# Forming the low parts of four weight units of each mixer on GpSimd in place of VectorE, in a two-layer hybrid backbone on one Trainium2 core

## The reference

```
p_ctx = h_ctx @ w_in
p_lat = h_lat @ w_in
...
z_c, xs_c, b_c, c_c, dtr_c = ssm_inputs(p_ctx[..., o2:], conv_w, conv_b)
...
out_lat = jnp.concatenate([oa_l, ob_l, oc_l], axis=-1)
...
xl = xl + ml[5] * (mix_l @ w_out[l])
```

## Time and profile before

| | |
|---|---|
| median of 3 runs | 1856.92 us (1856.59 to 1858.24) |
| the profiled execution's own time | 1856.45 us |
| its span, first to last instruction | 1854.7 us |
| busy: PE, PEld, DVE, ACT, POOL | 1802.6 (97%), 1490.1 (80%), 1426.0 (77%), 750.3 (40%), 59.8 us (3%) |
| mean granted TensorE clock | 0.976 |
| PE's waits for the mixer's low parts (L961) | 9.1 us, in 3 waits, the longest 4.4 us |

### The profile page before, as it was taken

The page is one execution under the profiler, slowest core; times in us unless marked ns, Lnnn a source line. Parts: engine busy times, 40 slices in busy tenths (PEclk is TensorE's granted clock), DMA queues, the critical chain, the costliest instruction groups (busy, mean ns, idle before and its releaser), DMA issues.

```text
span 1854.7 us, 26139 instructions
## 1 busy us (share of the span) xinstructions
PE 1802.6 (97%) x9314; PEld 1490.1 (80%) x9314; DVE 1426.0 (77%) x2351; ACT 750.3 (40%) x1146; POOL 59.8 (3%) x104
## 2 busy tenths in 40 slices
PE   8999999999999899999999999999999998899999
PEld 5788888886776577888888888888888687599999
DVE  6899977889786767777878678777786988757665
ACT  4322222247745657222222362222224765754342
POOL 1000000000000000000000010000000000000000
PEclk8999999999998899999999999999999999979999
DMA  8445544413312023444443233444440323025542
GB/s 356 178 178 205 196 165 158 176 72 124 126 46 91 1 91 137 152 165 158 153 178 144 91 137 142 178 155 158 158 157 26 137 75 148 13 114 185 193 172 107
DMA packets 37587, 259.50 MB, mean 140 GB/s; under 512 B 4369, under 2 KB 5841, under 8 KB 7441
## 3 DMA queue, kind: packets, MB, share of 16 engines
q1 hardware_dynamic: 26066, 182.32, 26.9%
q0 software_dynamic: 11456, 76.32, 11.2%
HBM read 252.60 MB, written 5.24 MB: 139 GB/s over the span
## 4 chain that ended last, share of the span: by engine, by line
PE 87%; ACT 5%; DVE 5%; issue 2%; DMA 1%; POOL 0%; DVEq 0%; ACTq 0%; SPq 0%; POOLq 0%
PE ps L1559 25%; PE ps L1560 25%; PE ps L1561 25%; PE ps L1663 2%; PE ps L1871 1%; ACT w_hi L566 1%; PE ps L1599 1%; ACT n_t L617 1%; PE ps L1595 1%; DVE cv L1276 1%; DMA scale_w<-scale_in 1%; PE ps L1932 1%; PE ps L1836 1%; DVE w_lo L961 1%; PE ps L1685 1%
## 5 line engine op out<-in xcount | busy, mean ns | idle before, releaser
L1559 PE MATMUL ps<-h_hi,w_hi 128*128 128x512 f32 (+2 forms) x1792 | 661.9, 369 | 14.7 <-DVE w_lo L961 9.1
L1560 PE MATMUL ps<-h_lo,w_hi 128*128 128x512 f32 (+2 forms) x1792 | 654.4, 365 | 0.0
L1561 PE MATMUL ps<-h_hi,w_lo 128*128 128x512 f32 (+2 forms) x1792 | 653.7, 365 | 0.0
L1559 PEld LDWEIGHTS ps<-h_hi,w_hi 128*128 128x128 f32 (+1 forms) x1792 | 341.0, 190 | 76.7 <-issue 11.0
L1560 PEld LDWEIGHTS ps<-h_lo,w_hi 128*128 128x128 f32 (+1 forms) x1792 | 341.1, 190 | 54.9 <-issue 1.4
L1561 PEld LDWEIGHTS ps<-h_hi,w_lo 128*128 128x128 f32 (+1 forms) x1792 | 340.9, 190 | 55.1
L956 DVE TENSOR_TENSOR w_lo<-raw,w_hi 128x2048 fp32r<-128x2048 f32 x132 | 302.0, 2288 | 83.1 <-ACT w_hi L566 83.0
L1084 DVE SCALAR_TENSOR_TENSOR x_res<-ps,abg,x_res 128x256 f32<-128x256 f32 x584 | 248.6, 478 | 140.9 <-PE ps L1561 139.4
L566 ACT ACTIVATE w_hi<-raw 128x2048 fp32r<-128x2048 f32 x129 | 246.6, 1911 | 258.7 <-PE ps L1561 256.7
L979 DVE CUSTOM_DVE_ANT_0 mod_prod<-mod_raw,cb 128x1024 f32<-128x1024 f32 x256 | 301.5, 1220 | 0.2 <-DVE mod_t L983 0.2
L1559 PE MATMUL ps<-a_hi,w_hi 128*128 128x512 f32 (+1 forms) x640 | 233.2, 364 | 5.6 <-DVE x_res L1084 5.6
(11 more groups left out here) (238 smaller groups left out, 1698.2 us busy)
## 6 DMA issues: line engine op xcount, KB each, us to landing
raw<-ffn_in SPq DMA_DIRECT2D x132, 1024.0 KB, 4.8
mod_raw<-mod_in POOLq DMA_DIRECT2D x68, 1024.0 KB, 5.0
raw<-proj_in SPq DMA_DIRECT2D x20, 1024.0 KB, 4.8
raw<-out_w_in SPq DMA_DIRECT2D x8, 1024.0 KB, 4.9
x_spill<-x_res SPq DMA_DIRECT2D x2, 2048.0 KB, 8.0
x_res<-x_spill SPq DMA_DIRECT2D x2, 2048.0 KB, 8.3
scale_w<-scale_in POOLq DMA_DIRECT2D x4, 512.0 KB, 12.8
x_res<-x_in SPq DMA_DIRECT2D x2, 1024.0 KB, 11.6
```

The source lines that it names most:

```text
L1559: pe.matmul(dst, w_hi[:, slot, wsl], hi, start=first, stop=False)
L1560: pe.matmul(dst, w_hi[:, slot, wsl], lo, start=False, stop=False)
L1561: return pe.matmul(dst, w_lo[:, slot, wsl], hi, start=False, stop=last)
```

## The change

The low parts of units 3, 4, 5 and 6 of both mixers are taken out of VectorE's stream and put into GpSimd's, in `mixer_rows`: two ahead of the DMA of the decay totals and two behind it. Each waits for the unit's high part and for the low part before it. VectorE's low part of unit 7 waits for `lo_ready` to count unit 6.

```diff
+POOL_LOWS = (3, 4, 5, 6)
...
+            def low_parts(layer, units):
+                for m in units:
+                    pool.wait_ge(hi_ready, mix_base(layer) + m + 1)
+                    pool.wait_ge(lo_ready, mix_base(layer) + m)
+                    pool.tensor_tensor(w_lo[:, m % 3, :], raw[:, m % 2, :], w_hi[:, m % 3, :], ALU.subtract).then_inc(lo_ready, 1)
+
             def mixer_rows(layer):
...
                 if layer == 0:
                     pool.memset(st[:, 2:4, :], 0.0).then_inc(st_zero, 1)
+                low_parts(layer, POOL_LOWS[0:2])
                 pool.wait_ge(row_act, ROW_ACTS * (layer + 1))
                 pool.dma_start(tot_dram[layer], lam[0:16, 72:76]).then_inc(tot_out, 16)
+                low_parts(layer, POOL_LOWS[2:4])
                 pool.wait_ge(cv_ready, 6 * (layer + 1))
...
             def split_mix(layer, m):
+                if m in POOL_LOWS:
+                    return
                 n = P if m == DT_UNIT else UNIT
                 dve.wait_ge(hi_ready, mix_base(layer) + m + 1)
+                if m - 1 in POOL_LOWS:
+                    dve.wait_ge(lo_ready, mix_base(layer) + m)
                 tt(w_lo[:, m % 3, 0:n], raw[:, m % 2, 0:n], w_hi[:, m % 3, 0:n], ALU.subtract).then_inc(lo_ready, 1)
```

## The result

The changed kernel takes **1877.95 us** (median of 4 runs, 1877.16 to 1879.30) beside 1856.76 us for the kernel before on the same chip (4 runs, 1855.86 to 1858.24). The ratio is **1.0106, 95% interval 1.0092 to 1.0120**: slower by 21.2 us where 13.4 were forecast. The span of the profiled execution is 1876.2 us against 1854.7, the mean granted clock 0.973 against 0.976; PE is still busy for 96% of the span.

A forecast was written before the change was run, and what follows sets the result against it. PE, busy for 97% of the span, was taken to bound the kernel, so only its idle time counts. 3.6 + 6.8 + 3.0 = +13.4 us on the median gives 1870.3 us, range 1858 to 1880 us.

The forecast's parts named there:

- The lock: Mixer heads: a VectorE instruction with two SBUF inputs waits out any GpSimd instruction reading SBUF, and the reverse.
- Rival 1: Mixer heads: no lock for this instruction, VectorE gains 2.29 us per low part; about 1852.8 us, faster; chance 10%.
- Rival 2: Mixer heads: GpSimd needs under some 2.5 us per low part; 0 to +3 us, about 1858 us; chance 12%.
- Rival 3: Mixer heads: a waiting GpSimd gets the lock only when VectorE runs idle; some +29 us, 1886 us; chance 8%.
- The price of one low part: Mixer heads: one low part on GpSimd takes 3.8 us, two passes over the tile, between 1.89 and 5.7 us.
- term 1: First mixer's head: PE starts tile 7 at 466.7 against 463.04, waiting for an evacuation and a low part; +3.6 us.
- term 2: Second mixer's head: PE starts tile 8 at 1493.4 against 1486.64, behind a late evacuation; +6.8 us.
- term 3: Second mixer's head: PE's added waits bring one more stretch of 6.2 us at half clock; +3.0 us, between 0 and 3.
- What costs nothing: First mixer: unit 6's low part has 5.1 us of slack and GpSimd's DMAs queue some 6 us later, without loss.
- The rest of what costs nothing: First mixer: `etb` is read over 20 us behind its issue, the library load hides in GpSimd's idle time; no loss.

The follow-up runs named there:

- e3: Kernel before, all low parts on VectorE, plus a useless GpSimd subtraction behind the fourth, fifth and sixth high parts of each mixer; 1879.64 us, ratio 1.0116.
- e4: Kernel before, all low parts on VectorE, plus three useless GpSimd memsets behind the same three high parts of each mixer; 1859.42 us, ratio 1.0013.
- e7: Kernel before, all low parts on VectorE, plus two useless one-input GpSimd copies behind the same three high parts of each mixer; 1873.53 us, ratio 1.0082.
- e1: The change with unit 6's low part back on VectorE, only units 3, 4 and 5 on GpSimd; 1871.61 us, ratio 1.0072 to the kernel before.
- e2: Kernel before with only unit 6's low part of each mixer moved to GpSimd; 1864.88 us, ratio 1.0035.
- e9: Kernel before with the convolution's middle tap formed on ScalarE for four of six channel tiles, nothing on GpSimd; 1863.30 us, ratio 1.0019.
- e5: Kernel before with only unit 6's low part on GpSimd and all six row transfers behind VectorE's eighth low part; 1875.80 us, ratio 1.0094.
- e6: The change with each GpSimd low part split into four subtractions of 512 columns; 1872.67 us, ratio 1.0074 to the kernel before.
- e8: Kernel before with only unit 6's low part on GpSimd, two `etb` transfers ahead of it, four wide ones behind VectorE's eighth; 1866.81 us, ratio 1.0055.

## Why the prediction was right in sign and short in size

- **The lock** was right. The steps of VectorE with two SBUF tiles as inputs that run beside a GpSimd row last about as long as that row, in both mixers, and e3, e4 and e7 show that reading SBUF on GpSimd does it, not lateness, not GpSimd's being busy. Its condition was too narrow: TENSOR_SCALAR steps, which read one SBUF tile, are held as well (L1337, 4.76 us for 0.48, is the first step that the change stops, where the prediction had put the scan). Rivals 1, 2 and 3 did not come: no step with two SBUF tiles as inputs kept its length (L1298 at 495.75, which has one of its two tiles in PSUM, did, inside GpSimd's row from 492.16 to 496.78), GpSimd took 4.6 us and not under 2.5, and it started 0.08 us behind its high part (445.58 behind 443.60 + 1.90 on ScalarE).
- **The price of one low part** was mis-sized: 4.6 us, where I took 3.8 between bounds of 1.9 and 5.7. The Trainium skill's page GPSIMD Engine Reference, in Performance versus the Vector engine, gives 4.5 us; the trace agrees with it (4.51 to 4.71) and not with my two passes.
- **First mixer, term 1**: tile 7 starts at 468.92, which is 467.75 less the 1.17 us by which that execution was late from its start, against 463.04: +4.7 for +3.6. **Second mixer, term 2**: when the second mixer begins, the changed kernel is 11.30 us late (GpSimd's memset of `rows`, 1467.37 for 1456.07), so tile 8's 1505.81 is 1494.51 against 1486.64: +7.9 for +6.8. The price explains more than what was missing: between the prediction's own points for 3.8 and 5.7 us, a price of 4.6 would give +5.2 and +9.0. Tile 7 of the second mixer was foretold for 1486.1 and is at 1486.80.
- **The clock, term 3**: what the second head lost behind tile 8's start is 10.28 - 7.9 = 2.4 us in the change, 9.30 - 7.9 = 1.4 in e1 (whose tile 8 starts at 1499.66, and which comes to the second mixer 5.17 us late), for +3.0. The granted clock agrees: 6.2 us at 0.56 cost 6.2 x 0.44 = 2.7 us in the change, and at e1's 0.73 they cost 1.7.
- The errors of the three terms cancel: e1, which has all that they speak of, is at +13.4 in its heads and in its median. There tile 7 is 4.7 us late, 0.6 of it is made up before the first `z`, tile 8 is 7.9 late and 1.4 are lost behind it, for 3.6, 6.8 and 3.0. That the sum is met to a tenth of a microsecond is luck. It is luck in part, too, that the change's 1877.95 us lies in the range of 1858 to 1880: the upper end stands for a price of 5.7 us, and what brings the time near it is a cost that the prediction put at nothing.
- **What costs nothing** is the step that failed. The low part of unit 6 lies 5.1 us ahead of its use, that was so, and PE never waits for it. But its end also frees `raw`, and I did not follow that line to SP: the load of unit 8 begins later, runs beside the DMAs that I had let "queue behind four low parts" for nothing, takes 7.20 us for 4.8, and holds ScalarE's stream. Beside e1, which lacks unit 6, the change loses 19.7 - 13.4 = 6.3 us more in the heads, 5.3 of them in the first mixer (9.40 for 4.07): PE waits 3.38 us there, and its granted clock is 0.76 from 508 to 515, where the kernel before has 1.00. The stop that e2 shows in the second mixer is not among them: in the change GpSimd's row there, from 1516.79 to 1521.40, falls into idle time of VectorE, the 6.07 us ahead of 1522.60. The other 1.0 us is the lower clock behind tile 8's start, 0.56 for 0.73, ahead of that row; nothing shows that unit 6 causes it.
- **The rest of what costs nothing** did cost nothing that a row shows, though the slack of `etb` was smaller than I had it: the program waits for it ahead of L1367, at 507.49 in the kernel before, and not only ahead of its reader at 516.74. In the change no such wait shows. For the library load, GpSimd's first low part starts 0.08 us behind its high part.

## What to carry to other kernels

Before giving GpSimd work to relieve VectorE, list what VectorE does beside it: if those steps have two SBUF inputs (here also if they are TENSOR_SCALAR steps with one) and GpSimd's instruction reads SBUF, VectorE stops for the length of GpSimd's instruction, and at 4.6 us for 2.29 the trade loses even where GpSimd is idle. When a step is moved, follow every semaphore that it raises, the buffer it frees and the load behind that too, not only the consumer of its result; and look at which DMAs its new place pushes into that load. If such work must go to GpSimd, short pieces can cost less than one long instruction (ratio 1.0074 against 1.0106 here, all of it gained in the second mixer).

## What was not expected of the hardware

**TensorE's clock in the attention.** With the same work, the stretch from the first `z` to the cast takes 135.8 us in the profiled execution of the kernel before and 143.9 in that of e9. The stretch of 21 us that begins 62 us behind the first `z`, in the kernel before and in e9 (columns as in the earlier trace rows):

```profile
633.11:654.11 21.00, 20.09 (x112) 11.62 (x111) 13.90 (x46) 13.36 (x39) 0.00 (x0) 1.00 0.00 1
```

```profile
631.93:652.93 21.00, 20.22 (x66) 11.01 (x65) 9.13 (x31) 10.38 (x28) 0.00 (x0) 0.53 0.00 0
```

PE is busy for 20 of 21 us in both; the granted clock is 1.00 in one and half in the other, which does fewer matmuls by 46. Just ahead PE had been idle for about 0.9 us in both, so the idle time alone does not tell them apart. e9's 12 executions fall into two groups, 4 from 1856.01 to 1857.32 us and 8 from 1863.00 to 1865.64, and the +8.11 us of its profiled one (1863.15 us) would make that gap; the first group is 1.6 us under the 1858.18 of the kernel before, near the -1.7 us of the heads. That each group has its own clock is inferred, since one execution of each kernel is profiled. The kernel before has the longer time as well, but seldom: of its 49 executions on record one took 1865.61 us, and no other more than 1859.66. e5, e6 and e8 show the same loss in the first mixer (6.8 to 8.3 us), with a clock of 0.51 to 0.54 in the same stretch and again 0.9 us of idle time ahead, and six kernels lose 3.8 to 6.7 us in the second. So a gain of 1 or 2 us ahead of the attention can be followed by a larger loss in it; whether the one causes the other, and what decides, stays open.

**A subtraction's price.** GpSimd took 3.60 to 4.02 us in e3, with one float32 tile as both inputs and a float32 output, and 4.51 to 4.71 us for `raw` minus `w_hi` with an fp32r output. Which of these differences makes the 0.9 us was not tried.
